# Three of a decoder layer's four norm statistics by a square matrix of ones instead of row sums, transposition and spread

## The reference

```python
def rms_norm(x, g):
    return x * lax.rsqrt(jnp.mean(x * x, axis=-1, keepdims=True) + EPS) * g

mod = jax.nn.silu(c) @ ada_w + ada_b
sh1, sc1, g1, sh2, sc2, g2 = jnp.split(mod, 6, axis=-1)
h = rms_norm(x, norm1_g) * (1 + sc1) + sh1             # norm 1, RMS
y = conformer_conv(h, ...)     # GLU, causal depthwise conv of 31 taps, LayerNorm (norm 2), silu, pointwise
x = x + g1 * y
h = rms_norm(x, norm2_g) * (1 + sc2) + sh2             # norm 3, RMS
x = x + g2 * (jnp.square(jax.nn.relu(h @ w1)) @ w2)    # 2048 -> 8192 -> 2048
return rms_norm(x, final_g)                            # norm 4, RMS
```

## Time and profile before

| | us |
|---|---|
| runs, median of 3 | 2128.62 |
| lowest, highest | 2123.72, 2129.82 |
| the profiled execution, own time | 2129.86 |
| its span, first to last instruction | 2128.1 |
| PE busy in it | 2004.2 (94%) |
| DVE busy | 1097.9 (52%) |
| ACT busy | 667.8 (31%) |
| POOL busy | 451.1 (21%) |
| mean granted TensorE clock | 0.968 of 2.4 GHz |

### The profile page before, as it was taken

How to read it: one execution, slowest core, us unless ns; L and a number is a source line. 1 busy time by engine, 2 the same in 40 slices (tenths; PEclk the granted TensorE clock), 3 DMA queues, 4 the chain that set the end, 5 groups by cost and what they waited for, 6 DMA issues and landing times.

```text
span 2128.1 us, 22314 instructions
## 1 busy us (share of the span) xinstructions
PE 2004.2 (94%) x8640; PEld 1632.2 (77%) x8640; DVE 1097.9 (52%) x1133; ACT 667.8 (31%) x717; POOL 451.1 (21%) x197
## 2 busy tenths in 40 slices
PE   5889999888987889999999999999999999999996
PEld 2668888656766767888888888888888888888885
DVE  5959989978698984323323332332332332232243
ACT  4334545453232222232132123123213213312332
POOL 3647999923433230000000000000000000000001
PEclk8999999979998999999999999999999999999998
DMA  9962433315866572222222222222222222222212
GB/s 399 394 258 101 158 138 118 119 60 197 341 262 246 202 292 91 87 99 99 99 99 99 99 87 91 100 96 99 99 99 99 99 99 80 101 95 99 99 59 79
DMA packets 45933, 299.58 MB, mean 141 GB/s; under 512 B 4688, under 2 KB 4688, under 8 KB 10960
## 3 DMA queue, kind: packets, MB, share of 16 engines
q1 hardware_dynamic: 45904, 299.24, 37.5%
HBM read 295.03 MB, written 4.19 MB: 141 GB/s over the span
## 4 chain that ended last, share of the span: by engine, by line
PE 72%; DVE 13%; POOL 6%; issue 4%; DMA 3%; ACT 2%; SPq 0%; DVEq 0%; POOLq 0%; ACTq 0%
PE ps L313 23%; PE ps L314 23%; PE ps L315 23%; DVE adar L760 3%; POOL wlo L1055 3%; DMA adar<-ada 3%; DVE adar L772 2%; DVE raw L772 1%; POOL pacc L1094 1%; DVE hlo L766 1%; PE ps L386 1%; DVE ps L843 1%; POOL adar L1098 1%; DVE wlo L783 1%; ACT whi L472 1%
## 5 line engine op out<-in xcount | busy, mean ns | idle before, releaser
L313 PE MATMUL ps<-hhi,whi 128*128 128x512 f32 (+1 forms) x1792 | 708.6, 395 | 61.7 <-DVE hlo L766 29.8
L314 PE MATMUL ps<-hlo,whi 128*128 128x512 f32 (+1 forms) x1792 | 704.9, 393 | 0.0
L315 PE MATMUL ps<-hhi,wlo 128*128 128x512 f32 (+1 forms) x1792 | 704.4, 393 | 0.0
L472 ACT ACTIVATE whi<-raw 128x2048 fp32r<-128x2048 f32 x176 | 336.1, 1910 | 680.5 <-PE ps L315 680.5
L313 PEld LDWEIGHTS ps<-hhi,whi 128*128 128x128 f32 x1792 | 341.4, 191 | 141.0 <-issue 56.2
L313 PE MATMUL ps<-dhi,whi 128*128 128x512 f32 x1024 | 399.8, 390 | 11.7 <-DVE dlo L1020 11.7
L314 PE MATMUL ps<-dlo,whi 128*128 128x512 f32 x1024 | 399.6, 390 | 0.0
L315 PE MATMUL ps<-dhi,wlo 128*128 128x512 f32 x1024 | 399.3, 390 | 0.0
L315 PEld LDWEIGHTS ps<-hhi,wlo 128*128 128x128 f32 x1792 | 340.9, 190 | 72.2
L314 PEld LDWEIGHTS ps<-hlo,whi 128*128 128x128 f32 x1792 | 341.6, 191 | 70.7
L783 DVE TENSOR_TENSOR wlo<-raw,whi 128x2048 fp32r<-128x2048 f32 x127 | 291.0, 2292 | 95.6 <-ACT whi L472 95.6
(11 more groups left out here) (142 smaller groups left out, 951.3 us busy)
## 6 DMA issues: line engine op xcount, KB each, us to landing
raw<-w SPq DMA_DIRECT2D x176, 1024.0 KB, 4.8
adar<-ada SPq DMA_DIRECT2D x80, 1024.0 KB, 5.0
raw<-ada SPq DMA_DIRECT2D x16, 1024.0 KB, 8.5
xb<-xT SPq DMA_DIRECT2D x8, 1024.0 KB, 9.6
out<-xb SPq DMA_DIRECT2D x5, 512.0 KB, 4.3
out<-xb SPq DMA_DIRECT2D x6, 256.0 KB, 3.8
csb<-c SPq DMA_DIRECT2D x1, 1024.0 KB, 4.9
pr<-par SPq DMA_DIRECT2D x1, 368.0 KB, 14.3
```

Source lines behind the costliest of these rows:

```text
L313: pe.matmul(out, whi[:, slot, t], xhi, start=first, stop=False, skip_group_check=True)
L314: pe.matmul(out, whi[:, slot, t], xlo, start=False, stop=False, skip_group_check=True)
L315: return pe.matmul(out, wlo[:, slot, t], xhi, start=False, stop=last, skip_group_check=True)
L472: act.activation(whi[:, q % WS, :], raw_slot(q), ACT.Copy).then_inc(whi_done, 1)
```

## The change

It gives norms 1, 3 and 4 another way to the same numbers. Norm 2 keeps its own. With a 128x128 matrix of ones, `onesq`, as weights, a matmul on a squared tile leaves the sum over partitions for each of the 512 tokens on every one of the 128 partitions (`all_sums`). ACT takes the root of the whole bank, with scale 1/D and bias epsilon, and DVE the reciprocal of 128x512. So transposition, the 128x4 statistics and the spread are gone. At norms 3 and 4 the last square is not added to `ssum` on DVE: PE takes `ssum` after fifteen additions and the last square as a second matmul. At norm 4 the reciprocal is taken twice, once into `rstd` for POOL and once into PSUM bank 1 for DVE. `ones`, `g1b`, `dump` and `eps` become slices of tiles that are there.

```diff
-        ones = sb("ones", [P, 1])
+        onesq = sb("onesq", [P, P])
+        ones = onesq[:, 0:1]
...
+            def all_sums(bank, src, start, stop):
+
+                return pe.matmul(ps[:, bank, :], onesq[:], src, start=start, stop=stop, skip_group_check=True)
...
-                last = pe.matmul(ps[0:1, 6, :], ones[:], x_squares[k % 2][:], start=k == 0, stop=k == KC - 1,
-                                 skip_group_check=True)
-                last.then_inc(xsq_used, 1)
-            pe.wait_ge(row_copied, 1)
-            for j in range(T // P):
-                last = pe.matmul(ps[:, 5, j:j + 1], ta[0:1, j * P:(j + 1) * P], ones[0:1, :], start=j == 0,
-                                 stop=False, skip_group_check=True)
-            last.then_inc(stat_done, 1)
-            pe.wait_ge(ident_set, 1)
+                all_sums(6, x_squares[k % 2][:], k == 0, k == KC - 1).then_inc(xsq_used, 1)
             pe.wait_ge(root_done, 1)
-            spread(7, 8)
-
-            pe.wait_ge(rstd_done, 1)
             outer_units(A0, 0)
...
-            pe.wait_ge(ss1_done, KC)
-            token_sums(2, 0, ssum, True).then_inc(stat_done, 1)
-            pe.wait_ge(root_done, 3)
-            spread(3, 8)
+            pe.wait_ge(ss1_done, KC - 1)
+            all_sums(2, ssum[:], True, False)
+            pe.wait_ge(x1sq_done, KC)
+            all_sums(2, sq[:], False, True).then_inc(stat_done, 1)
...
-            pe.wait_ge(ss2_done, KC)
-            token_sums(0, 0, ssum, True).then_inc(stat_done, 1)
-            pe.wait_ge(root_done, 4)
-            spread(1, 8)
+            pe.wait_ge(ss2_done, KC - 1)
+            all_sums(0, ssum[:], True, False)
+            pe.wait_ge(x2sq_done, KC)
+            all_sums(0, ta[:], False, True).then_inc(stat_done, 1)
...
+            def root(out, bank):
+
+                act.activation(out[:], ps[:, bank, :], ACT.Sqrt, scale=1.0 / D, bias=eps).then_inc(root_done, 1)
...
             act.wait_ge(xsq_used, KC)
-            act.activation(ta[0:1, :], ps[0:1, 6, :], ACT.Copy).then_inc(row_copied, 1)
+            act.wait_ge(eps_set, 1)
+            root(ta, 6)
             split_hi(0)
-            root(1, 7)
...
             x1_square(15)
+            act.wait_ge(stat_done, 1)
+            root(ta, 2)
             split_hi(C0 + 1)
-            root(3, 3)
...
-            root(4, 1)
+            act.wait_ge(stat_done, 2)
+            root(tb, 0)
...
-            dve.wait_ge(stat_done, 1)
+            dve.wait_ge(root_done, 1)
+            dve.reciprocal(rstd[:], ta[:]).then_inc(rstd_done, 1)
             dve.memset(pacc[:, 0:2], 0.0).then_inc(conv_done, 1)
-            variance(5)
...
-            add_squares(15, ss1_done, x1sq_done)
...
-            dve.wait_ge(stat_done, 2)
-            variance(2)
+            dve.wait_ge(root_done, 3)
+            dve.reciprocal(rstd[:], ta[:]).then_inc(rstd_done, 1)
...
-                add_squares(2 * m + 1, ss2_done, x2sq_done, ta)
+                if m < BLK - 1:
+                    add_squares(2 * m + 1, ss2_done, x2sq_done, ta)
+            dve.wait_ge(root_done, 4)
+            dve.reciprocal(rstd[:], tb[:]).then_inc(rstd_done, 1)
+            dve.reciprocal(ps[:, 1, :], tb[:]).then_inc(stat_done, 1)
+            dve.wait_ge(fg_done, KC)
             dve.wait_ge(stat_done, 3)
-            variance(0)
-            dve.wait_ge(fg_done, KC)
-            dve.wait_ge(rstd_done, 5)
```

More of the change, by code:

```diff
@@ L75, in trunk_kernel @@
         b1p = sb("b1p", [P, 2 * KC])
-        g1b = sb("g1b", [P, KC])
+        g1b = b1p[:, 0:KC]
         st = sb("st", [P, 16])
-        ones = sb("ones", [P, 1])
+        onesq = sb("onesq", [P, P])
+        ones = onesq[:, 0:1]
         ident = sb("ident", [P, P])
-        dump = sb("dump", [P, 1])
+        tiny = sb("tiny", [P, 2])
+        dump, eps = tiny[:, 0:1], tiny[:, 1:2]
         with ExitStack() as between:
@@ L130, in trunk_kernel @@
         out_done = sem("out_done")
+        eps_set = sem("eps_set")
         ones_set, ident_clear, ident_set = sem("ones_set"), sem("ident_clear"), sem("ident_set")
@@ L139, in trunk_kernel @@
         mod_sum = sem("mod_sum")
-        row_done = sem("row_done")
-        row_copied = sem("row_copied")
         scaled_done = sem("scaled_done")
@@ L344, in token_sums @@
                 for j in range(T // P):
-                    last = pe.matmul(ps[:, bank, col0 + j:col0 + j + 1], src[:, j * P:(j + 1) * P], ones[:],
+                    last = pe.matmul(ps[:, bank, col0 + j:col0 + j + 1], src[:, j * P:(j + 1) * P], ones,
                                      start=start and j == 0, stop=False, skip_group_check=True)
@@ L398, in _ @@
                 token_sums(0, 4, sig if c % 2 else sq, False).then_inc(ln_used, 1)
+            pe.wait_ge(ident_set, 1)
             pe.wait_ge(root_done, 2)
@@ L476, in preload @@
                 act.wait_ge(ones_set, 1)
[L477 to L488, removed]
+                act.activation(dump, ones, func).then_inc(warm, 1)
+            def root(out, bank):
+                act.activation(out[:], ps[:, bank, :], ACT.Sqrt, scale=1.0 / D, bias=eps).then_inc(root_done, 1)
             def h_hi(k, n, src):
@@ L620, in _ @@
                 c_square(c)
-            root(2, 1, 2)
+            act.wait_ge(var_done, 1)
+            act.activation(st[:, 8:12], st[:, 4:8], ACT.Sqrt).then_inc(root_done, 1)
+            preload(ACT.Silu)
+            act.wait_ge(spread_done, 1)
+            act.activation(rstd[:], ps[:, 1, :], ACT.Copy).then_inc(rstd_done, 1)
+            act.wait_ge(spread_done, 2)
+            act.activation(mu[:], ps[:, 2, :], ACT.Copy).then_inc(rstd_done, 1)
             def z(k):
@@ L745, in chain @@
                 dve.wait_ge(dv, steps[0])
-            dve.memset(ones[:], 1.0).then_inc(ones_set, 1)
+            dve.memset(onesq[:], 1.0).then_inc(ones_set, 1)
+            dve.memset(eps, EPS).then_inc(eps_set, 1)
             dve.wait_ge(par_in, 16)
@@ L751, in _ @@
             dve.tensor_scalar(b1p[:, KC:2 * KC], col("ada_b", M_SC2, KC), 1.0, None, ALU.add).then_inc(small, 1)
-            def variance(bank):
-                chain(dve.tensor_scalar(st[:, 0:4], ps[:, bank, 0:4], 1.0 / D, EPS, ALU.mult, ALU.add))
-                dve.reciprocal(st[:, 4:8], st[:, 0:4]).then_inc(var_done, 1)
             def ada_reduce(a, off=0):
@@ L914, in gate1 @@
                 dve.wait_ge(small, n_small + 1)
-                dve.tensor_tensor(g1b[:], modb[:, M_G1:M_G1 + KC], col("b_out", 0, KC), ALU.mult
+                dve.tensor_tensor(g1b, modb[:, M_G1:M_G1 + KC], col("b_out", 0, KC), ALU.mult
                                   ).then_inc(small, 1)
```

## The result

| us | before | changed |
|---|---|---|
| median of 8 runs each | 2128.65 | 2134.40 |
| lowest, highest | 2123.72, 2131.60 | 2132.32, 2138.87 |
| profiled execution: own time, span | 2129.86, 2128.1 | 2134.62, 2132.8 |

The ratio is 1.0030, 95% interval 1.0018 to 1.0042, or 6.4 us; the medians differ by 5.75 us and the two profiled spans by 4.7. It is a small loss. The forecast was +3.8 us, 2132.4, in a range of 2124 to 2138.

What follows compares the result with a forecast made beforehand. The prediction took PE to bound the MLP and DVE's queue to bound A0, C0 and the tail. Norm terms +2.1 - 1.0 + 2.7 gave +3.8 us, forecasting 2132.4 us in a range of 2124 to 2138.

Steps and rivals of the forecast that it cites:

- within 0.3%: Whole kernel: time differs from before by no more than about 0.3%, or 6.4 us; chance 0.73.
- The reciprocal's price: DVE's reciprocal on 128x512 was taken to last 3.0 us, with 0.69 and 4.0 us as ends.
- 17 ns over four elements: DVE's 128x4 reciprocal exceeds a tensor-tensor by 17 ns; read as 4.3 ns per element, giving 2.9 us on 128x512.
- Norm 1: Ahead of A0: DVE's next adaLN row and `scale_x` start 2.1 us later, and A0 keeps the delay.
- Norm 3: Ahead of C0: small DVE operations run without POOL, so the first multiplication starts 1.0 us sooner.
- a shift of its first multiplication is carried to its end: In C0, a shift of DVE's first multiplication reaches the stage's end, since multiplications and adaLN rows share one queue.
- Norm 4: In the tail: DVE's first multiplication starts 2.7 us later, after two reciprocals, and the end moves with DVE.
- The cheap reciprocal: Rival at all three norms: the reciprocal takes 0.69 us, sum -4.2, 2124.4 us; chance 0.10.
- The dear one: Rival ahead of A0 and in the tail: reciprocal 4.0 us or more, +6.8, 2135.4 us; border 3.87 us; chance 0.22.
- PE's passes keep the clock up: Rival at norms 3 and 4: the clock stays up and both chains shorten, sum +1.2, 2129.8 us; chance 0.10.
- the reciprocal shuts POOL out: Rival at norm 3: POOL's split waits for DVE's reciprocal, +0.2 there, sum +5.0, 2133.6 us; chance 0.08.
- The mark set for the forecast's failure: The forecast is wrong if A0 takes back the 2 us, or C0 does not end earlier relative to A0.

Runs made afterwards that it cites:

- run 9: The changed kernel measured again, unmodified: 2134.65 us, ratio 1.0027 to the kernel before.
- Run 1: The changed kernel with all four 128x512 reciprocals replaced by plain copies, so the output is scaled wrongly: 2123.84 us, ratio 0.9974 to the kernel before.
- Run 6: The changed kernel with ACT's order at norm 3 as before, the weight split ahead of the root: 2137.33 us, ratio 1.0038 to the kernel before.
- run 2: The changed kernel with norm 4's second reciprocal, into PSUM, replaced by a copy of rstd: 2130.46 us, ratio 1.0006 to the kernel before.
- run 10: The kernel before with norms 3 and 4 as in the change, norm 1 as before: 2129.65 us, ratio 1.0007.
- runs 8: The kernel before with only the tiles of the change, all norms as before: 2129.30 us, ratio 0.9995.
- 11: The kernel before, unmodified, profiled again in a single execution: 2129.18 us.
- run 7: The changed kernel with Ln and Exp on ACT in place of root and reciprocal at norms 1 and 4: 2123.53 us, ratio 0.9971 to the kernel before.

## Why the prediction was right

**The sum.** Forecast +3.8 us. Measured are +5.75 by the medians and 6.4 by the ratio, and in run 9 6.5 and 5.7. Time and range held, "within 0.3%" holds with the ratio at its border, and the loss has the forecast's places and signs. The sum was low by 2 us or somewhat more. By place:

- *The reciprocal's price* was mis-sized: 3.0 us taken, 3.35 measured. Three of them are on the path, 1.05 us. The reading of 17 ns over four elements pointed the right way: the slope is 6.25 ns, against 5.3 with equal fixed parts and 7.5 at the upper end. The Trainium skill (VectorE: DVE Perf Modes, the section on the 8-slice pipeline) gives a repeat count of 8, from which 4.3 us were estimated. Measured are 6.25 ns per element, six cycles of 0.96 GHz and not eight; here the measurement decides. Run 1 shows that the reciprocals carry the loss.
- *Norm 1*: +2.1 forecast, +3.2 in the two profiles, 2.9 as the mean difference of the first column (the five profiles with the new norm 1 and its reciprocal against the seven with the old). Besides the reciprocal, the wider loads were 1.0 us at the root's start where 0.5 was taken. That A0 keeps it was right: its end moved from 141.21 to 144.27.
- *Norm 3*: -1.0 forecast, -1.1 in the profiles. The chain was as described, four passes mostly at half clock, small operations freed, the multiplication held by POOL. Run 6 shows the cause. The step behind it was wrong: "a shift of its first multiplication is carried to its end". C0 takes the 1.1 us back on the way to an adaLN row that waits for its load, and in run 1, of 6.7 us ahead of the kernel before at the second multiplication, 3.0 were left at the last adaLN row. What the change gained there instead, some 3 us, came by the order of one pair, which the prediction did not have. That C0 gained anything near the forecast was luck.
- *Norm 4*: +2.7 forecast, +3.9 measured. 0.7 of the 1.2 is the reciprocal and 0.1 the root, 0.69 us for 0.6; the sums ended 0.4 us later than worked out: the first two passes took 1.22 us to the start of the next where 0.86 was taken, with a load of 128 columns that showed and the clock at half before they were through. That the end moves with DVE was right (run 2).

**The rivals.** The cheap reciprocal is run 1's kernel in effect, and there the change would have gained. The dear one lies above the measured price; its border of 3.87 us was not reached, though the other terms brought the loss to about 0.3%. That PE's passes keep the clock up did not happen in seven of the eight tails with the new sums, nor at norm 3; in run 10 it did. Two of six tails with the old sums kept the full clock too, so no run shows that the passes are what holds it. That the reciprocal shuts POOL out is refuted by the overlap at 682.07. The mark set for the forecast's failure, C0 not ending earlier relative to A0, did not occur: it ended 2.2 us earlier relative to A0's end (3.1 us late there, 0.9 at the last adaLN row), but by the meeting and not by the path that the forecast had.

**Left open:** norm 1, C0's usual form and norm 4 together give about 2.9 - 3.2 + 3.9 = +3.6 us, the two series 5.7 to 6.4 with some 2.5 us of uncertainty each way, and the parts measured alone give less still. Between A0's end and the last x1 the executions differ by up to 3 us (527.3 to 530.2), also where the code there is the same, and which part of that follows the change was not settled. The MLP is not quite the same length either: in runs 8, 10 and 11, the three whose tail kept the full clock, it took 1.5 us more from the last adaLN row to the last update of x (1316.7 against 1315.2). Why stays open.

## What to carry to other kernels

Before a small statistic is widened to a whole tile to save transposition and spread, price every operation at the width it will have: what is 178 ns on four elements may be 3.35 us on 512, and on an engine's full queue it is paid in whole. Look next for what stands beside the statistics, because at norm 3 the gain at its place came from moving one POOL operation out of the way of a tiny DVE one. Then follow a gain to the end of its stage: here the loads of the adaLN rows took it back. Where two engines exclude each other, an order that is decided by a few hundredths of a microsecond can be worth more than the edit, so look at several profiles before a difference of 0.1% is explained.

## What the runs showed of the hardware

- A reciprocal of 128x512 on DVE takes 3.35 us from SBUF to SBUF and 3.30 into PSUM, 6.25 ns per element beyond 178 ns at four. It runs beside a POOL tensor-tensor: 4.50 us for the split that started inside it.
- A DVE operation on 128x16 with two SBUF inputs took 4.34 us beside a POOL split already running; its own time is 0.17. The other way round, a POOL split that started 0.03 us behind a DVE row took 6.71 us instead of 4.61.
- Weights of 128 columns that alternate with ACT's squares show 0.1 us in every second pair of passes (1.13 against 1.02 us), and at norms 3 and 4 the granted clock fell to half within four passes that PE had begun at the full clock (1.00 to 0.50 at 2109.5); in run 10's tail, with the same code, it stayed at 1.00.
- Between Ln and Exp stands a table load of 1.28 us in run 7, at norm 1 and in the tail.
